# Sharing the finish of the last row tile between VectorE, ScalarE and GpSimd in a hybrid attention layer

## The reference

```
h = rmsnorm(x, norm_pre_g)
u = h @ w_in                              # 1024 x 4096
a, b = differential attention, block-sparse attention on slices of u, each gated by SiLU
y = concat(a, b) @ w_out                  # 1024 x 1024
out = x + rmsnorm(y, norm_post_g)

def rmsnorm(x, g, eps):
    ms = mean(x * x, axis=-1)
    return x * rsqrt(ms + eps) * g
```

## Time and profile before

| What | Value |
|---|---|
| median of 3 runs | 254.14 us (254.02 to 254.44) |
| time of the profiled execution | 254.23 us |
| its span, first to last instruction | 252.4 us |
| TensorE busy | 245.6 us, 97% of the span |
| VectorE busy | 177.0 us, 70% |
| ScalarE busy | 143.0 us, 57% |
| GpSimd busy | 32.7 us, 13% |
| granted TensorE clock, mean | 0.997 of full speed |

### The profile page before, as it was taken

How to read it: one execution, slowest core, us unless ns; L and a number is a source line. 1 busy time by engine, 2 the same in 40 slices (tenths; PEclk the granted TensorE clock), 3 DMA queues, 4 the chain that set the end, 5 groups by cost and what they waited for, 6 DMA issues and landing times.

```text
span 252.4 us, 4450 instructions
## 1 busy us (share of the span) xinstructions
PE 245.6 (97%) x1567; PEld 123.2 (49%) x1567; DVE 177.0 (70%) x393; ACT 143.0 (57%) x336; POOL 32.7 (13%) x74
## 2 busy tenths in 40 slices
PE   8999999999999999999999999999999999999991
PEld 6454444445444554544455444454444444555570
DVE  2998585587478688868877767977787896835313
ACT  4777565375356666574677595667565665611110
POOL 1329300000000320041031033000000000111101
PEclk9999999999999999999999999999999999999998
DMA  6978979605656545544935644568849869982422
GB/s 242 366 245 173 310 251 371 218 28 135 106 160 163 180 114 130 140 163 112 203 103 136 137 161 119 136 189 184 174 103 201 209 157 170 202 203 43 125 86 83
DMA packets 59674, 42.47 MB, mean 168 GB/s; under 512 B 45808, under 2 KB 46072, under 8 KB 59652
## 3 DMA queue, kind: packets, MB, share of 16 engines
q1 hardware_dynamic: 59636, 42.18, 63.5%
q10 hardware_dynamic: 16, 0.00, 0.0%
HBM read 29.04 MB, written 2.13 MB: 123 GB/s over the span
## 4 chain that ended last, share of the span: by engine, by line
PE 97%; DVE 1%; DVEq 0%; POOLq 0%; issue 0%; ACT 0%; POOL 0%; ACTq 0%
PE unit_ps L578 72%; PE score_ps L634 6%; PE o_ps L655 5%; PE unit_ps L608 4%; PE unit_ps L589 3%; PE unit_ps L615 2%; PE unit_ps L543 1%; PE score_ps L536 1%; PE score_ps L709 1%; PE unit_ps L709 1%; DVE area L1058 0%; DVE gates L956 0%; DVEq L180 0%; POOLq L180 0%; ACT junk L732 0%
## 5 line engine op out<-in xcount | busy, mean ns | idle before, releaser
L578 PE MATMUL unit_ps<-area,w_hi 128*128 128x512 f16 x256 | 76.2, 379 | 0.0
L788 ACT ACTIVATE arena<-arena,negmax 128x512 f32<-128x512 f32 (+3 forms) x64 | 35.4, 554 | 49.5 <-DVE negmax L985 49.4
L578 PE MATMUL unit_ps<-w_hi,area 128*128 128x512 f16 x192 | 60.3, 379 | 0.0
L578 PE MATMUL unit_ps<-area,w_lo 128*128 128x512 f16 x128 | 48.5, 379 | 0.0
L578 PEld LDWEIGHTS unit_ps<-area,w_hi 128*128 128x128 f16 x256 | 24.1, 98 | 27.2 <-issue 1.1
L578 PE MATMUL unit_ps<-w_lo,area 128*128 128x512 f16 x96 | 36.4, 379 | 0.0
L985 DVE CUSTOM_DVE_ANT_0 arena<-score_ps,strips 128x512 f32<-128x512 f32 (+3 forms) x64 | 28.6, 485 | 9.2 <-PE score_ps L634 9.2
L882 DVE SCALAR_TENSOR_TENSOR w_lo<-stage,g_cols,w_hi 128x512 f16<-128x512 f32 x32 | 24.2, 755 | 11.3 <-ACT w_hi L746 11.2
L578 PEld LDWEIGHTS unit_ps<-w_hi,area 128*128 128x128 f16 x192 | 18.8, 98 | 21.9 <-DVE w_lo L888 0.7
L745 ACT ACTIVATE w_hi<-stage,g_cols 128x512 f16<-128x512 f32 x32 | 22.7, 711 | 7.3 <-DMA stage<-in_w_in_dram 7.3
L884 DVE SCALAR_TENSOR_TENSOR w_lo<-stage,g_cols,w_hi 128x512 f16<-128x512 f32 x32 | 24.8, 777 | 0.0
(11 more groups left out here) (106 smaller groups left out, 357.7 us busy)
## 6 DMA issues: line engine op xcount, KB each, us to landing
stage<-in_w_in_dram SPq DMA_DIRECT2D x32, 512.0 KB, 4.3
stage<-in_w_out_dram SPq DMA_DIRECT2D x8, 512.0 KB, 4.2
arena<-in_x_dram SPq DMA_DIRECT2D x4, 512.0 KB, 5.2
strips<-bias_rows SPq DMA_DIRECT2D x4, 512.0 KB, 4.7
stage<-in_x_dram SPq DMA_DIRECT2D x4, 512.0 KB, 4.7
out_dram<-area SPq DMA_DIRECT2D x3, 512.0 KB, 2.7
strips<-bias_rows SPq DMA_DIRECT2D x1, 1024.0 KB, 7.8
pt<-arena SPq DMA_TRANSPOSE x32, 3.1
```

The costliest lines, as they stand in the source:

```text
L578: last = nc.tensor.matmul(bank, a, b, start=(k == 0 and n == 0), stop=(k == KT - 1 and n == 2))
L788: nc.scalar.activation(probs[:, i % 2, m, 0:n], probs[:, i % 2, m, 0:n], ACT.Exp, bias=negmax[:, i, m:m + 1], scale=-1.0, accum_out=sums[: ...
```

## The change

The last row tile is no longer finished by VectorE alone. VectorE makes columns 0 to 383 and 384 to 767 in two passes. ScalarE multiplies columns 768 to 1023 by `y_rstd` in place, and GpSimd adds the residual to them. The two stores become 384 columns (192 KB) and 640 columns (320 KB); the second also waits for GpSimd's part. The last addition of the sum of squares, before at line 524 on GpSimd, becomes VectorE's, ahead of `weigh_half(1)`. GpSimd keeps the power.

```diff
+    LAST_PARTS = [slice(0, 3 * DM // 8), slice(3 * DM // 8, 3 * DM // 4)]
+    SHARED = slice(3 * DM // 4, DM)
+    LAST_STORES = [LAST_PARTS[0], slice(3 * DM // 8, DM)]
...
@ sync
-            for half in range(2):
-                cols = slice(half * WIDTH, (half + 1) * WIDTH)
-                sp.wait_ge(y_ready, TILES + half)
+            for part, cols in enumerate(LAST_STORES):
+                sp.wait_ge(y_ready, TILES + part)
+                if part == 1:
+                    sp.wait_ge(shared_ready, 1)
                 sp.dma_start(out_v[TILES - 1][:, cols], y_sb[:, (TILES - 1) % 2, cols]).then_inc(stored_last, 16)
@ gpsimd
                     nc.gpsimd.tensor_tensor(y_most[:, :], y_sq[:, t, 1:2], y_part[:, t:t + 1],
                                             ALU.add).then_inc(y_most_ready, 1)
-                    pool.wait_ge(y_most_ready, 1)
-                    pool.wait_ge(y_squared, Y_UNITS + 1)
-                    nc.gpsimd.tensor_tensor(y_ms[:, t:t + 1], y_sq[:, t, 2:3], y_most[:, :],
-                                            ALU.add).then_inc(y_mean, 1)
                 pool.wait_ge(y_mean, i + 1)
                 nc.gpsimd.tensor_tensor(y_rstd[:, t:t + 1], y_ms[:, t:t + 1], minus_half[:, 0:1],
                                         ALU.pow).then_inc(y_rstd_ready, 1)
+            t = TILES - 1
+            pool.wait_ge(xres_loaded[t], 16)
+            pool.wait_ge(shared_scaled, 1)
+            nc.gpsimd.tensor_tensor(y_sb[:, t % 2, SHARED], y_sb[:, t % 2, SHARED], stage[:, t, SHARED],
+                                    ALU.add).then_inc(shared_ready, 1)
@ scalar, at the end
+            act.wait_ge(y_weighted, Y_UNITS + 1)
+            act.wait_ge(y_rstd_ready, TILES)
+            nc.scalar.activation(y_sb[:, (TILES - 1) % 2, SHARED], y_sb[:, (TILES - 1) % 2, SHARED], ACT.Copy,
+                                 scale=y_rstd[:, TILES - 1:TILES]).then_inc(shared_scaled, 1)
@ vector, finish_rows
-                parts = 1 if t < TILES - 1 else 2
+                parts = [slice(0, DM)] if t < TILES - 1 else LAST_PARTS
...
-                for part in range(parts):
-                    cols = slice(part * DM // parts, (part + 1) * DM // parts)
+                for cols in parts:
@ vector, at the end
             weigh_half(0, unit_ps[:, LAST_UNIT % 2, 0:WIDTH // 2])
+            dve.wait_ge(y_most_ready, 1)
             dve.wait_ge(y_squared, Y_UNITS + 1)
+            nc.vector.tensor_tensor(y_ms[:, TILES - 1:TILES], y_sq[:, TILES - 1, 2:3], y_most[:, :],
+                                    ALU.add).then_inc(y_mean, 1)
             weigh_half(1, score_ps[:, 0, 0:WIDTH // 2])
             finish_rows(TILES - 1)
```

More of the change, by code:

```diff
@@ L342, in bass_hymba_diff_moba_layer @@
         y_ready = sem("y_ready")
+        shared_scaled = sem("shared_scaled")
+        shared_ready = sem("shared_ready")
         diff_normed = sem("diff_normed")
```

## The result

The changed kernel takes 254.72 us (median of 20 runs, 254.12 to 255.84) against 254.14 us of the kernel before (20 runs, 253.69 to 254.58). The ratio is 1.0023, with a 95% interval of 1.0013 to 1.0032: 0.58 us more, with 0.33 to 0.81 in the interval. That is at the edge of what a measurement of this kernel can tell from no change. The forecast was 254.4 with a range of 253.95 to 254.95.

A forecast was written before the change was run, and what follows sets the result against it. The end was taken as bound by when the stores are issued and 512 KB at full rate. Plus 0.34 us (0.21 in the other order), taken as 0.30, gave 254.4 from a median of 254.14; range 253.95 to 254.95.

The forecast's parts named there:

- Where the time goes: Everything the change touches lies in the last 5.5 us, after TensorE stops; nothing is changed before 247.4.
- The sum on VectorE: Last addition of the sum of squares: GpSimd's power starts at 247.68 instead of 247.82, gaining 0.14 us.
- VectorE's passes, ScalarE's scaling, GpSimd's addition: Last row tile's finish: 0.62 us per 384-column pass, 0.50 for scaling 256 columns, 0.73 for adding 256 without interference.
- The straight line: Estimate of GpSimd's 256-column addition, 0.73 us, drawn between 0.19 for one column and 1.27 for 512.
- The meeting: VectorE's second pass and GpSimd's addition exclude each other at SBUF; VectorE goes first, GpSimd ends 0.59 later, at 250.08.
- The other order: GpSimd goes before VectorE's second pass: GpSimd ends at 249.54, VectorE at 249.95, in total plus 0.21 us.
- The row at 113.14: Earlier trace row where GpSimd won although VectorE began 0.03 earlier; cited against the start deciding who goes first.
- The second store: Last store, 320 KB: issued at 250.11 against 249.92, its data ending at 251.80 against 251.46, plus 0.34 us.
- The sum: Total of the end's steps: plus 0.30 us, between plus 0.34 and plus 0.21, or 0.12% more.
- Beside each other: Rival: GpSimd's addition isn't held by VectorE's passes and ends at 249.65; minus 0.09 us, chance 0.15.
- A much slower addition: Rival: GpSimd's addition takes far more than 0.73 us; plus 0.5 to 0.9, upper bound 255.0, chance 0.18.
- ScalarE late: Rival: ScalarE's scaling comes late, changing the order but not the time, plus 0.34; included in the 0.60 for taking turns.

The follow-up runs named there:

- the share of 128 columns: Changed kernel with GpSimd and ScalarE sharing 128 columns in place of 256, VectorE making 448 and 448; 254.47 us, ratio 1.0009 to the kernel before.
- the two experiments where GpSimd led by 0.06 and 0.09: Changed kernel with a share of 128 columns (254.47 us), and with 256 shared but VectorE passes of 576 and 192 (254.31 us); both ratio 1.0009.
- the experiment with PSUM: Changed kernel with the last row tile's weighed columns 0 to 767 kept in PSUM, two stores; 254.41 us, ratio 1.0 to the kernel before.
- the sum alone: Kernel before with only the last addition of the sum of squares moved to VectorE; 254.28 us, ratio 0.9998, and 254.06 us, ratio 1.0008 in a second set.
- the pass of 576: Changed kernel with the 256-column share kept but VectorE passes of 576 and 192 columns; 254.31 us, ratio 1.0009 to the kernel before.

## Why the prediction was right, and where its size was off

**Where the time goes.** Right. The code ahead of S is the same, and the end grew by 0.40. TensorE played no part.

**The sum on VectorE.** Right in direction, half in size. I took 0.14 us; VectorE's finish starts 1.46 after S in place of 1.54, so 0.08. The addition starts at 248.03, 0.10 after ScalarE's sum is out at 247.93, where I had taken the 0.04 of the weighing; why it took longer, no run shows. The link to the power, 248.19 to 248.27, is the 0.08 of the forecast.

**VectorE's passes, ScalarE's scaling, GpSimd's addition.** 0.62, 0.51 and, by itself, 0.72 us, against 0.62, 0.50 and 0.73. The straight line between one column and 512 held; the share of 128 columns gave 0.46, where it gives 0.46. ScalarE started with VectorE (248.91, 248.92) and not 0.06 ahead of it.

**The meeting.** This was the main step and it held: GpSimd ends 0.57 after VectorE's second pass (250.64 - 250.07), forecast 0.59, in the order that I had taken. Taking the meeting away gave back 0.35. That the order came out so is in part luck: the rows before left it open, I took a lead of 0.05 us for VectorE, and in the two experiments where GpSimd led by 0.06 and 0.09 it turned round. The other order would have been plus 0.21, still within the range. By the rule of the Trainium skill (SBUF — State Buffer, "Who interferes with whom") whoever starts first keeps the inputs; the three leads here agree, by the recorded starts. The row at 113.14 that I held against it stays unexplained.

**The second store.** The larger piece cost 0.11 on its own, and 0.14 between the experiment with PSUM and the sum alone, which both issue it 2.91 after S; the bytes say 0.17 (64 KB more at 1.38 us for 512). The issue came 3.26 after S (250.72 - 247.46), forecast 250.11 - 246.93 = 3.18. Of these 0.08, 0.03 are GpSimd's end (the sum 0.06 late, the work behind it 0.03 shorter), and 0.05 are SP, which issued 0.08 after GpSimd and not 0.03 as after VectorE.

I had left the time from the end of the data to the end of the span as it was and named a change of it with the size of the last store as a sign of being wrong. By the packet records it is 0.85 us before and 0.84 in the changed kernel, and 0.83 to 0.85 behind every last store of 224 to 320 KB (my 0.94 was counted from busy shares). Behind the smaller last stores of the experiments it is longer, 0.90 at 192 KB and 0.99 to 1.03 at 128 KB. For this change the step held; in general it doesn't.

**The sum.** The forecast was plus 0.34 for this order, of which I took 0.30. The end measured plus 0.40 and the times plus 0.58 (0.33 to 0.81). So the mechanism was right and the size 0.10 short in the end: 0.04 that I had cut off towards the order that didn't happen, and 0.08 in the issue of the store, less 0.02 in its data and behind it. The 0.18 between 0.40 and 0.58 lie inside the interval and are not explained by a row. Laid out from the runs: minus 0.09 for the sum, plus 0.11 for the larger last store, plus 0.35 for the meeting make 0.37, against 0.40.

**The rivals.** Beside each other: fell, by the 1.08. A much slower addition: fell, by the 0.72. ScalarE late: it was 0.1 late and cost nothing, as GpSimd waited for VectorE anyway. I had forecast no measurable change; the measured ratio lies a hair above my bound of 0.2%, and the interval on both sides of it. By itself the 0.58 lies in the band that I had given to a slower addition (plus 0.5 to 0.9); that this rival is not the cause is told by the rows, not by the time. The upper bound of that rival was worked out as 255.0, and the range should have reached it instead of ending at 254.95. The chance of 0.23 for slower was rather low for a sum that already stood at 0.34 of the 0.51 us that decide.

## What to carry to other kernels

Before work is given to another engine, lay its whole chain beside the work saved: here 0.51 on ScalarE, two hand-overs and 0.72 on GpSimd stood against 0.26 us of VectorE, and even free of any meeting came out even. Look for rows in which the two engines already met at the same inputs; one such row is worth more than their separate durations. And a store that waits for a late part should be a small one: that won 0.31 us where GpSimd was late. A third store won nothing where the last part wasn't late, as its issue came 0.10 to 0.13 later and the time behind its data was longer.

## What the runs showed of the hardware that was not expected

GpSimd's recorded start can lie ahead of the end of VectorE's pass without a wait. In the share of 128 columns it starts at 248.56, 0.15 before VectorE's first pass ends at 248.71, and still takes its free 0.46; with 256 columns behind the pass of 576 it started 0.18 before 248.84 and took 0.76 in place of 0.72. That fits the rule taken from the kernel before, that the one who waits ends its own duration less 0.14 behind the other: 0.31 and 0.58 here. Whether GpSimd needs its inputs only after its recorded start, or VectorE is through with them before its recorded end, the rows can't tell.

A pass of VectorE can be long without having work: 0.88 us for 192 columns, as long as the 448 columns took in the same place. Read as a duration it would be 4.6 ns a column; beside GpSimd's row it is a wait.

Issues of stores that follow closely on each other cost more. Those that started 0.07 and 0.04 us after the one ahead had ended took 0.43 and 0.45 us; all others at the end of these kernels, at least 0.19 apart, took 0.33.
